# Two of the eight last output tiles made by POOL from a second laying-out of the roots, and the values of the second mixers turned three steps later

## The chip, the cores and the metric

The kernel runs on one core of one Trainium2 chip. The metric is device time in microseconds: lower is better. All times in this document are microseconds unless marked ns. The engines are PE (TensorE, matmuls; PEld are its weight loads), DVE (VectorE), ACT (ScalarE), POOL (GpSimd) and SP (SyncE, which issues most DMAs here).

## What is computed

Two transformer blocks in fp32 on 512 tokens of width 1024. The first is one layer: a mixer with windowed attention and neighborhood attention, then a squared-relu MLP. The second has two layers, each a half-step SwiGLU MLP, a mixer (`c0`, `c1`) of sliding-window attention with a sink beside a short convolution, and a second SwiGLU MLP. Two parts matter for this change, the attention's input and the last norm:

```python
h = rms_norm_2(x, mix_norm[l])
z = h @ w_in[l]
q, k, v = z[..., :Q_END], z[..., Q_END:K_END], z[..., K_END:V_END]
...
p = jnp.where(mask_b, jnp.exp(scores - m), 0.0)
out = jnp.einsum("bnkgqs,bnskd->bnqkgd", probs, v_band)
...
def rms_norm_2(x, gain):
    inv = lax.rsqrt(jnp.mean(x * x, axis=-1, keepdims=True) + NORM_EPS)
    return (x * inv) * gain
return rms_norm_2(x, final_norm)
```

## The kernel before

**Layout.** x lies in SBUF with the features on the partitions: eight tiles `x[:, m, :]` of 128 features by 512 tokens, and the output leaves in the same form. Every dense product is made of three passes per 128x128 piece of weights: w_hi by h_hi, w_hi by h_lo, w_lo by h_hi (lines 769 to 771, 128x512 each), where hi and lo are the two parts into which a value is split. A result is 8 such steps (24 matmuls) into one of three PSUM banks. Weights come by DMA in units of 512 KB; ACT makes w_hi (line 894), DVE makes w_lo (line 1091).

**What sets the order.** The class `Plan` writes one list of jobs, and each engine's program walks that list and emits its own part of each job, so every engine works strictly in list order. `dense` calls `next_slot` after each step, and `later(n, job)` puts a job n slots (steps of three matmuls) on. The engines are held together only by semaphores.

**The second mixers.** `second_mixer` begins with `qkv_gqa(s, 9)`: a result for the keys (`stack` k), one for the values (`project_v`), and four for the queries (`stack` 0 to 3). For each stack DVE scales the bank by the root of the norm into a buffer z (line 1083), ACT copies two or four halves as the high part (line 940), and DVE subtracts them for the low part (line 1158). For the values DVE scales into z (1083), PE turns z by four transposes of 128x128 against the identity into a bank (job `v_turn`, line 833), and ACT copies that bank to v (line 956). The second argument of `qkv_gqa`, 9, is the number of slots from the end of the values' result to the turn. PE's transposes wait for the semaphore `evacuated` of the values' z. In the second mixers' attention PE makes scores (line 783) into two banks in turn, and DVE takes them out with the distance bias (line 1270, semaphore `biased`); the third score of a group waits until the first is taken out.

**The end.** Job `output`: PE sums the squares of each token into four columns (lines 854, 857), ACT takes the root (`token_root`, line 1052), DVE inverts it (1305) and spreads it by the identity into four 128x128 blocks of a z (1310). PE multiplies each block by ones (line 862), which lays the inverse roots out over all partitions in a PSUM bank, `score_bank[0]`. DVE then makes the eight output tiles in place, x times gain times that bank (line 1314), and SP issues one DMA of 256 KB for each as its tile is ready (line 1447). SP then waits until all have landed.

Of the kernel before, what the change touches and what calls it, by code (L numbers as in the profile page):

```python
# [32 lines left out]
Z_RING = 5  # L33
WARMING = 11
GRID_W = 64
GRID_R = TOKENS // GRID_W
# [71 lines left out]
class Plan:  # L108
# [20 lines left out]
        "neg_sinks": ("neg_sinks",), "rel_bias": ("rel_spread",), "far_1": (), "far_2": (),  # L129
        "warm_root": (), "output": ("norm_summed", "rooted", "inverted"),  # L130
    }
# [291 lines left out]
    def second_mixer(self, layer):  # L423
        s, name = 3 + 3 * layer, f"c{layer}"
        self.phase_result[s] = len(self.results) - 1
        self.add("far_2", layer)
        self.add("pad_conv", layer)
        self.pending_norm = s
        self.qkv_gqa(s, 9)
        self.split_job = "split_g"  # L430
        self.attend(name, 5, 10, 11)
        for f in range(4):
            key = (layer, f)
            self.add("conv_c", key, self.dense_h(s))
            r = self.dense_h(s)
            self.add("conv_h", key, r, self.z("conv_u", key))
            self.later(3, "conv_own", *key)
            self.later(5, "conv_earlier", *key)
            r = self.dense_h(s)
            self.add("conv_b", key, r, self.z("project_lo", key))  # L440
            self.later(3, "conv_hi", *key)
        self.finish_beside()
        self.split_job = "split_v"
        self.out_projection(("cat", layer), s + 1)
        self.pending_norm = s + 1
# [82 lines left out]
def two_blocks(nc, dram, out):  # L528
    stack = ExitStack()
    with stack:  # L530
# [85 lines left out]
        names = dict.fromkeys(name for of in Plan.SIGNALS.values() for name in of)  # L616
        signals = {name: signal(name) for name in [*names, "mm_done", "evacuated", "ones_set", "eps_set", "rel_cleared", "spread", "rms_spread", "output_done"]}
        landed = [signal(f"w_landed{i}", 16) for i in range(UNITS_HELD)]
# [129 lines left out]
        def tensor_program(engine):  # L748
# [4 lines left out]
            for job, key, r, zs in jobs:  # L753
# [96 lines left out]
                elif job == "output":  # L850
# [9 lines left out]
                    for b in range(BLOCKS):  # L860
                        pe.wait_ge(signals["spread"].s, b + 1)
                        engine.matmul(score_bank[0][:, block(b)], ones[:, :], z[zs[1] % Z_RING][:, block(b)],
                                      start=b == 0, stop=True, skip_group_check=True).then_inc(signals["rms_spread"].s, 1)

        v_result, v_buffer = {}, {}
# [4 lines left out]
        def scalar_program(engine):  # L870
# [13 lines left out]
            for job, key, r, zs in jobs:  # L884
# [165 lines left out]
                elif job == "output":  # L1050
                    act.wait_ge(*done("norm_summed", FINAL))
                    engine.activation(token_root[:, :], value_bank[:, 0:BLOCKS], ACT.Sqrt, bias=eps_col[:, :], scale=1 / D_MODEL).then_inc(signals["rooted"].s, 1)

        h_until, conv_buffer, merge_result = {}, {}, {}
# [16 lines left out]
        def vector_program(engine):  # L1071
# [21 lines left out]
            for job, key, r, zs in jobs:  # L1093
# [209 lines left out]
                elif job == "output":  # L1303
# [7 lines left out]
                    v.wait_ge(signals["rms_spread"].s, BLOCKS)  # L1311
                    for m in range(KT):
                        v.wait_ge(*x_is(FINAL, m))
# [21 lines left out]
        def gpsimd_program(engine):  # L1335
            pool = Once(engine)
            for job, key, r, zs in jobs:
# [34 lines left out]
                elif job == "mask_bias":  # L1372
# [9 lines left out]
                    for (a, b), sign, base, event in ((lower, 1, GRID_R - 1, "bias_half"), (upper, -1, (WIN_W - 1) * GRID_R, "bias_masked")):  # L1382
                        in_place = i == 1 and sign < 0
                        if sign < 0:
# [4 lines left out]
                                             pattern=[[0, 4], [sign * GRID_R, b - a], [0, GRID_R]], channel_multiplier=-sign).then_inc(signals[event].s, 1)  # L1389

                elif job == "merge_b":
                    m = key
# [15 lines left out]
        def sync_program(engine):  # L1408
# [18 lines left out]
            for job, key, r, zs in jobs:  # L1427
# [16 lines left out]
                elif job == "output":  # L1444
                    for m in range(KT):
                        sp.wait_ge(signals["output_done"].s, m + 1)
                        engine.dma_start(out[m * P:(m + 1) * P, :], x[:, m, :]).then_inc(out_stored.s, 16)
# [139 lines left out]
```

## Time and profile before

| | us |
|---|---|
| runs | 2527.48, 2526.25, 2525.29 |
| median | 2526.25 |
| profiled execution, whole | 2525.54 |
| profiled execution, span from first to last instruction | 2523.7 |
| PE busy in the span | 2496.8 (99%) |
| DVE, ACT, POOL busy | 1189.6, 947.5, 182.6 |
| mean granted TensorE clock | 0.998 |

The span is what the trace shows, and 1.84 of the profiled execution lie around it. A row of a timeline gives the start, the duration, the engine and line, output<-input, and in brackets how long the engine was idle before it and who released it. Rows of the chain of waits give start, length and what the end of the kernel hung on at that time. In the tables by stretch the granted clock is a share of full speed: 1.00 is 2.4 GHz and 0.50 is 1.2 GHz.

### The profile page before, as it was taken

Reading aid. Unit: us, or ns where it says so; the run is one execution under the profiler, and the core shown is the slowest. Engines: PE = TensorE matmul, PEld = TensorE weight load, DVE = VectorE, ACT = ScalarE, POOL = GpSimd, SP = SyncE. Lnnn points to the kernel's source line nnn. Section 1 sums busy time; section 2 is a strip of 40 time slices with the busy share of each in tenths; the row PEclk is TensorE's granted clock in tenths of the full one; section 3 lists DMA queues with packets and bytes.
Section 4 is the critical chain, followed back from the end, with each engine's and each line's share of the span. In section 5 each row is a group of like instructions: output and inputs, shape, how many; then the busy total and the mean of one; then the engine's idle time right before and its main releaser. Section 6 shows DMA issues by size and latency. Waiting matters only on the chain.

```text
span 2523.7 us, 28242 instructions
## 1 busy us (share of the span) xinstructions
PE 2496.8 (99%) x11504; PEld 2071.3 (82%) x11504; DVE 1189.6 (47%) x1595; ACT 947.5 (38%) x1398; POOL 182.6 (7%) x179
## 2 busy tenths in 40 slices
PE   9999999999999999999999999999999999999998
PEld 7878888888888888878888888888888788888887
DVE  6443454434475343454454444543444644544444
ACT  6668333322343232356432222422222464322222
POOL 2031010000020000011200000100000122000001
PEclk9999999999999999999999999999999999999999
DMA  7454433233223333245423332333332354332322
GB/s 197 109 124 118 134 108 100 92 100 101 92 84 109 93 99 94 89 130 130 115 95 100 93 99 89 99 97 99 94 101 87 112 142 117 100 99 93 100 90 78
DMA packets 78513, 265.33 MB, mean 105 GB/s; under 512 B 9648, under 2 KB 12976, under 8 KB 78000
## 3 DMA queue, kind: packets, MB, share of 16 engines
q1 hardware_dynamic: 69376, 233.57, 29.4%
q0 software_dynamic: 9008, 29.96, 6.0%
q8 instruction: 91, 1.49, 0.2%
q14 instruction: 38, 0.31, 0.0%
HBM read 234.56 MB, written 2.19 MB: 94 GB/s over the span
## 4 chain that ended last, share of the span: by engine, by line
PE 89%; DVE 4%; ACT 3%; issue 3%; POOL 0%; DMA 0%; SPq 0%; DVEq 0%; ACTq 0%; POOLq 0%
PE bank L769 28%; PE bank L770 28%; PE bank L771 28%; PE bank L810 2%; DVE w_lo L1091 2%; ACT w_hi L894 1%; PE bank L783 1%; PE bank L797 1%; DVE x L1207 1%; DVE z L1083 1%; ACT z L882 0%; POOL square_sum L1350 0%; DVE q L1158 0%; PE bank L843 0%; ACT h_hi L907 0%
## 5 line engine op out<-in xcount | busy, mean ns | idle before, releaser
L769 PE MATMUL bank<-h_hi,w_hi 128*128 128x512 f32 x2224 | 879.7, 396 | 2.7 <-DVE h_lo L1106 1.5
L771 PE MATMUL bank<-h_hi,w_lo 128*128 128x512 f32 x2224 | 867.2, 390 | 0.0
L770 PE MATMUL bank<-h_lo,w_hi 128*128 128x512 f32 x2224 | 867.0, 390 | 0.0
L1091 DVE TENSOR_TENSOR w_lo<-w_raw,w_hi 128x1024 fp32r<-128x1024 f32 (+2 forms) x392 | 485.3, 1239 | 318.3 <-ACT w_hi L894 317.9
L894 ACT ACTIVATE w_hi<-w_raw 128x1024 fp32r<-128x1024 f32 (+1 forms) x435 | 449.0, 1034 | 409.4 <-PE bank L771 407.3
L771 PEld LDWEIGHTS bank<-h_hi,w_lo 128*128 128x128 f32 x2224 | 417.9, 188 | 88.5
L769 PEld LDWEIGHTS bank<-h_hi,w_hi 128*128 128x128 f32 x2224 | 418.5, 188 | 86.9 <-DVE h_lo L1106 2.7
L770 PEld LDWEIGHTS bank<-h_lo,w_hi 128*128 128x128 f32 x2224 | 418.7, 188 | 80.8 <-issue 1.9
L769 PE MATMUL bank<-act_hi,w_hi 128*128 128x512 f32 x960 | 373.4, 389 | 0.0
L770 PE MATMUL bank<-act_lo,w_hi 128*128 128x512 f32 x960 | 373.4, 389 | 0.0
L771 PE MATMUL bank<-act_hi,w_lo 128*128 128x512 f32 x960 | 373.4, 389 | 0.0
L1083 DVE TENSOR_TENSOR z<-bank,rms_inv 128x512 f32<-128x512 f32 x238 | 168.6, 709 | 317.2 <-PE bank L771 316.1
L1207 DVE SCALAR_TENSOR_TENSOR x<-bank,x 128x512 f32<-128x512 f32 x152 | 104.6, 689 | 284.2 <-PE bank L771 284.2
L771 PEld LDWEIGHTS bank<-act_hi,w_lo 128*128 128x128 f32 x960 | 180.2, 188 | 37.5
L769 PEld LDWEIGHTS bank<-act_hi,w_hi 128*128 128x128 f32 x960 | 180.2, 188 | 37.5
L770 PEld LDWEIGHTS bank<-act_lo,w_hi 128*128 128x128 f32 x960 | 180.2, 188 | 37.1
L1350 POOL TENSOR_TENSOR square_sum<-square_sum,z 128x512 f32<-128x512 f32 x55 | 73.7, 1340 | 1839.5 <-ACT z L882 1839.5
L1014 ACT ACTIVATE act_hi<-z 128x512 fp32r<-128x512 f32 x88 | 55.6, 632 | 389.9 <-DVE z L1228 389.9
L1009 ACT ACTIVATE z<-z 128x512 f32<-128x512 f32 x88 | 55.6, 632 | 285.0 <-DVE z L1083 285.0
L1091 DVE TENSOR_TENSOR act_lo<-z,act_hi 128x512 fp32r<-128x512 f32 x120 | 83.1, 692 | 105.0 <-ACT act_hi L1014 61.4
L907 ACT ACTIVATE h_hi<-x,gains 128x512 fp32r<-128x512 f32 x56 | 40.6, 724 | 124.0 <-DVE x L1207 119.8
L1341 POOL DMA_DIRECT2D w_lo<-w_raw x51 | 44.3, 868 | 322.5 <-ACT w_lo L897 322.5
(169 smaller groups left out, 1676.8 us busy)
## 6 DMA issues: line engine op xcount, KB each, us to landing
w_raw<-ffn_wg_dram SPq DMA_DIRECT2D x88, 512.0 KB, 3.5
w_raw<-ffn_wu_dram SPq DMA_DIRECT2D x88, 512.0 KB, 3.5
w_raw<-w_in_dram SPq DMA_DIRECT2D x67, 512.0 KB, 3.6
w_raw<-ffn_wd_dram SPq DMA_DIRECT2D x64, 512.0 KB, 3.5
w_lo<-w_raw POOLq DMA_DIRECT2D x51, 512.0 KB, 4.4
w_raw<-w_up_dram SPq DMA_DIRECT2D x32, 512.0 KB, 3.5
w_raw<-w_down_dram SPq DMA_DIRECT2D x32, 512.0 KB, 3.5
w_raw<-w_out_dram SPq DMA_DIRECT2D x24, 512.0 KB, 3.5
```

Of the source, the lines that this page charges most:

```text
L769: engine.matmul(to, w_hi[s][:, lhs], hi, start=k == 0, stop=False)
L770: engine.matmul(to, w_hi[s][:, lhs], lo, start=False, stop=False)
L771: product = engine.matmul(to, w_lo[s][:, lhs], hi, start=False, stop=job == "k_last")
L810: product = engine.matmul(value_bank[:, half(place(name, h))], turned[0:rows, n * P:(n + 1) * P], values[name][0:rows, chunk, value_head(n ...
L894: engine.activation(w_hi[s][:, 0:width], w_raw[s][:, 0:width], ACT.Copy).then_inc(signals["w_hi"].s, 1)
L1009: engine.activation(z[zs[1] % Z_RING][:, :], z[zs[0] % Z_RING][:, :], ACT.Silu).then_inc(signals["silued"].s, 1)
L1014: engine.activation(act_hi[:, plan.hidden[key] % FF_RING, :], z[zs[1] % Z_RING][:, :], ACT.Copy).then_inc(signals["act_hi"].s, 1)
L1083: engine.tensor_tensor(to, src, scale, ALU.mult).then_inc(signals["evacuated"].s, 1)
L1091: engine.tensor_tensor(lo, value, hi.bitcast(F32), ALU.subtract).then_inc(signals[event].s, 1)
L1207: engine.scalar_tensor_tensor(x[:, m, :], dense_bank[plan.results[r].bank][:, :], factor(r), x[:, m, :], ALU.mult, ALU.add).then_inc(signa ...
L1341: engine.dma_start(w_lo[s][:, 0:width].bitcast(F32), w_raw[s][:, 0:width], accum_op=ALU.add).then_inc(signals[f"w_added{s}"].s, 16)
L1350: engine.tensor_tensor(to, to, z[zs % Z_RING][:, :], ALU.add).then_inc(signals["scaled_sum" if scaled else "square_sum"].s, 1)
```

## The change

Two independent edits. In the second mixers the turn of the values is put 12 slots behind their result, not 9. In the job `output`, after the four matmuls that lay the roots out for DVE, PE does the same four once more into `turn_bank[0]` and signals `rms_for_pool`. ACT, after its root, multiplies tiles 0 and 1 of x by their gains in place (`gained`), then copies the second bank to the SBUF tensor `rms_inv` (`root_copied`). POOL multiplies these two tiles by `rms_inv`, DVE makes only tiles 2 to 7, and SP issues the eight stores in the order 2, 3, 0, 4, 5, 1, 6, 7, each when its tile is signalled. The lines of the changed kernel are one to twenty further down (833 becomes 834, 862 becomes 863, 1314 becomes 1325, 1447 becomes 1467).

```diff
+BY_POOL = 2
@@ second_mixer
-        self.qkv_gqa(s, 9)
+        self.qkv_gqa(s, 12)
@@ tensor_program, job "output", behind the four matmuls of line 862
+                    pe.wait_ge(*turn_freed(len(plan.turns) - 1))
+                    pe.wait_ge(*turn_freed(len(plan.turns) - 2))
+                    for b in range(BLOCKS):
+                        spread = engine.matmul(turn_bank[0][:, block(b)], ones[:, :], z[zs[1] % Z_RING][:, block(b)],
+                                              start=b == 0, stop=True, skip_group_check=True)
+                    spread.then_inc(signals["rms_for_pool"].s, 1)
@@ scalar_program, job "output", behind the root
+                    for m in range(BY_POOL):
+                        engine.activation(x[:, m, :], x[:, m, :], ACT.Copy, scale=gains[:, 9, m:m + 1]).then_inc(signals["gained"].s, 1)
+                    act.wait_ge(signals["rms_for_pool"].s, 1)
+                    engine.activation(rms_inv[:, :], turn_bank[0][:, :], ACT.Copy).then_inc(signals["root_copied"].s, 1)
@@ vector_program, job "output"
-                    for m in range(KT):
+                    for m in range(BY_POOL, KT):
@@ gpsimd_program
+                elif job == "output":
+                    pool.wait_ge(*done("root_copied", FINAL))
+                    for m in range(BY_POOL):
+                        pool.wait_ge(signals["gained"].s, m + 1)
+                        engine.tensor_tensor(x[:, m, :], x[:, m, :], rms_inv[:, :], ALU.mult).then_inc(signals["output_done_g"].s, 1)
@@ sync_program, job "output"
-                    for m in range(KT):
-                        sp.wait_ge(signals["output_done"].s, m + 1)
+                    for m in (2, 3, 0, 4, 5, 1, 6, 7):
+                        if m < BY_POOL:
+                            sp.wait_ge(signals["output_done_g"].s, m + 1)
+                        else:
+                            sp.wait_ge(signals["output_done"].s, m - BY_POOL + 1)
                         engine.dma_start(out[m * P:(m + 1) * P, :], x[:, m, :]).then_inc(out_stored.s, 16)
```

On PE, in the mixer of the second block's first layer, the result that begins below is that of the second stack of queries. Before, with the semaphores that each row waits for:

```order
L769 MATMUL bank<-h_hi,w_hi 128x512 [waits evacuated,w_lo_v]
L770 MATMUL bank<-h_lo,w_hi 128x512
L771 MATMUL bank<-h_hi,w_lo 128x512
L769 MATMUL bank<-h_hi,w_hi 128x512
L770 MATMUL bank<-h_lo,w_hi 128x512
L771 MATMUL bank<-h_hi,w_lo 128x512
L833 MATMUL bank<-identity,z 128x128 [waits evacuated]
L833 MATMUL bank<-identity,z 128x128 x3
L769 MATMUL bank<-h_hi,w_hi 128x512
```

The four transposes stand behind the result's second step. In the changed kernel the same place, from the result's third step on:

```order
L770 MATMUL bank<-h_hi,w_hi 128x512
L771 MATMUL bank<-h_lo,w_hi 128x512
L772 MATMUL bank<-h_hi,w_lo 128x512
L770 MATMUL bank<-h_hi,w_hi 128x512
L771 MATMUL bank<-h_lo,w_hi 128x512
L772 MATMUL bank<-h_hi,w_lo 128x512
L770 MATMUL bank<-h_hi,w_hi 128x512
L771 MATMUL bank<-h_lo,w_hi 128x512
L772 MATMUL bank<-h_hi,w_lo 128x512
L834 MATMUL bank<-identity,z 128x128 [waits evacuated]
L834 MATMUL bank<-identity,z 128x128 x3
L770 MATMUL bank<-h_hi,w_hi 128x512
```

Nine matmuls now stand ahead of the transposes that stood behind them; the wait goes with the transposes. In the order of the work of ACT, DVE and POOL in the mixers nothing moves, the copy to v included.

On SP, the last rows of the program, the eight stores; before:

```order
L1417 DMA w_raw<-ffn_wd_dram 128x768 [waits w_lo_v] x8
L1447 DMA out_dram<-x 128x512 [waits output_done] x8
L530 UNCONDITIONAL_BRANCH [waits out_stored]
```

and in the changed kernel, where output_done comes from DVE and output_done_g from POOL:

```order
L1434 DMA w_raw<-ffn_wd_dram 128x768 [waits w_lo_v] x8
L1467 DMA out_dram<-x 128x512 [waits output_done] x2
L1467 DMA out_dram<-x 128x512 [waits output_done_g]
L1467 DMA out_dram<-x 128x512 [waits output_done] x2
L1467 DMA out_dram<-x 128x512 [waits output_done_g]
L1467 DMA out_dram<-x 128x512 [waits output_done] x2
L531 UNCONDITIONAL_BRANCH [waits out_stored]
```

The third store and the sixth now wait for POOL, with DVE's tiles queued behind them.

## Rows read from the trace of the kernel before

**Rows 1.** The page: busy us by engine, share of the span, instructions
```profile
PE 2496.8 (99%) x11504; PEld 2071.3 (82%) x11504; DVE 1189.6 (47%) x1595; ACT 947.5 (38%) x1398; POOL 182.6 (7%) x179
```
**Rows 2.** PE's waits: who for whom, total, times, longest
```profile
PE bank L783 <- DVE neg_max L1270: 7.6, 6, 3.5
PE bank L833 <- DVE z L1083: 2.1, 2, 1.0
```
**Rows 3.** Timeline, mixer of the second block's first layer, around the turn
```profile
1099.08 0.39 PE L771 MATMUL bank<-h_hi,w_lo 128*128 128x512 f32 x1
1099.74 0.69 DVE L1083 TENSOR_TENSOR z<-bank,rms_inv 128x512 f32<-128x512 f32 x1
...
1100.49 0.66 PE L833 MATMUL bank<-identity,z 128*128 128x128 f32 x4 [1.02 <-DVE z L1083]
...
1104.46 0.58 ACT L956 ACTIVATE v<-bank 128x512 f32<-128x512 f32 x1
...
1122.71 0.33 PE L783 MATMUL bank<-k_hi,q 128*128 128x128 f32 x1 [0.64 <-DVE neg_max L1270]
```
**Rows 4.** Chain of waits, same mixer: start, length, what the end hung on
```profile
1099.02 0.69 DVE k_lo L1158
...
1103.50 1.07 ACT w_hi L894
...
1121.58 0.69 DVE q L1158
...
1122.30 0.35 DVE probs L1270
```
**Rows 5.** PE's waits in the second layer's mixer, 1980 to 2100
```profile
PE bank L783 <- DVE neg_max L1270: 0.7, 1, 0.7
```
**Rows 6.** Timeline of PE: two long waits in the first mixer
```profile
53.71 0.38 PE L783 MATMUL bank<-ka_hi,qa 128*128 128x256 f32 x1 [3.48 <-DVE neg_max L1270]
104.30 0.66 PE L797 MATMUL bank<-identity,probs 128*128 128x128 f32 x4 [1.67 <-ACT probs_t L1038]
```
**Rows 7.** By stretch: time, busy of PE PEld DVE ACT POOL, clock, DMA share, GB/s
```profile
55.00:56.00 1.00, 0.89 (x3) 0.89 (x4) 0.52 (x5) 0.98 (x2) 0.13 (x1) 0.50 0.31 61
...
58.00:59.00 1.00, 1.00 (x5) 0.79 (x4) 0.00 (x0) 1.00 (x5) 0.00 (x0) 0.81 0.92 180
105.00:110.00 5.00, 5.00 (x34) 4.47 (x33) 3.81 (x9) 3.96 (x9) 0.86 (x1) 1.00 0.33 66
2515.80:2516.00 0.20, 0.13 (x2) 0.00 (x0) 0.03 (x1) 0.00 (x0) 0.00 (x0) 0.93 0.00 0
2517.30:2517.60 0.30, 0.00 (x0) 0.00 (x0) 0.30 (x2) 0.00 (x0) 0.00 (x0) 0.50 0.02 7
2519.00:2520.00 1.00, 0.00 (x0) 0.00 (x0) 1.00 (x3) 0.00 (x0) 0.00 (x0) 0.50 1.06 410
2522.60:2522.80 0.20, 0.00 (x0) 0.00 (x0) 0.00 (x0) 0.00 (x0) 0.00 (x0) 0.50 1.13 440
```
**Rows 8.** Timeline of the end, all engines
```profile
2513.76 0.26 ACT L1052 ACTIVATE token_root<-bank,eps_col 128x4 f32<-128x4 f32 x1 [1.14 <-PE bank L857]
...
2514.80 1.13 PE L862 MATMUL bank<-z,ones 128*128 128x128 f32 x8 [1.08 <-DVE z L1310]
2515.97 5.36 DVE L1314 SCALAR_TENSOR_TENSOR x<-x,gains,bank 128x512 f32<-128x512 f32 x8 [0.73 <-PE bank L862]
2516.74 4.94 SPq L1447 DMA_DIRECT2D out_dram<-x  x8
```
**Rows 9.** Line 1447: issue ns min/median/max, starts; us to landing
```profile
L1447 SPq DMA_DIRECT2D out_dram<-x x8: 332/333/348, 2516.7 to 2521.4; - x8
...
DMA to landing us min/median/max: 2.0/2.0/2.0
```
**Rows 10.** Groups by line: prices of the like work on ACT and POOL
```profile
L977 ACT ACTIVATE conv_y<-conv_u,conv_w 128x512 f32<-128x512 f32 x8 | 5.7, 708 | 0.0
L1406 POOL TENSOR_TENSOR z<-z,conv_y 128x512 f32<-128x512 f32 x8 | 10.3, 1289 | 37.5 <-DVE z L1083 37.5
```

More of the change, by code:

```diff
@@ L129 @@
         "neg_sinks": ("neg_sinks",), "rel_bias": ("rel_spread",), "far_1": (), "far_2": (),
-        "warm_root": (), "output": ("norm_summed", "rooted", "inverted"),
+        "warm_root": (), "output": ("norm_summed", "rooted", "inverted", "root_copied"),
     }
@@ L616, in two_blocks @@
         names = dict.fromkeys(name for of in Plan.SIGNALS.values() for name in of)
-        signals = {name: signal(name) for name in [*names, "mm_done", "evacuated", "ones_set", "eps_set", "rel_cleared", "spread", "rms_spread", "output_done"]}
+        signals = {name: signal(name) for name in [*names, "mm_done", "evacuated", "ones_set", "eps_set", "rel_cleared", "spread", "rms_spread", "rms_for_pool", "gained", "output_done", "output_done_g"]}
         landed = [signal(f"w_landed{i}", 16) for i in range(UNITS_HELD)]
```

## The prediction

> **What bounds the kernel now.** I read the page first. PE is busy for 2496.8 of 2523.7 [rows 1], so outside the last few microseconds time can come only from PE's waits or its work. The next view is the one of PE's waits, since it names what the first edit aims at: the transposes of line 833 wait twice for DVE's z (line 1083), 2.1 together, 1.0 the longest [rows 2]. Those are the turns of the values in the two second mixers. The same view has line 783 (scores) waiting for DVE's exit from the score banks, 7.6 in 6 waits. Two of these six turn out to matter: 0.64 at 1122.71, in the same mixer and 22 after the turn [rows 3], and 0.7 in the other layer's [rows 5]. So the third step was the chain of waits between the two places, and the fourth the timeline of the end. There PE has finished and the path is root, laying-out, eight DVE products, stores, landing [rows 8, 9].
>
> **Edit 1, the turn three steps later.** It adds and removes no instruction. Before, PE has nothing left to do in front of the transposes from 1099.47 (the last matmul starts at 1099.08 and takes 0.39) and waits 1.02 until z is out at 1100.43 (1099.74 + 0.69) [rows 3]. Now nine matmuls stand ahead. By the page a matmul costs 2496.8 / 11504 = 0.22 [rows 1], since they overlap, so they fill about 2.0, and PE reaches the transposes near 1101.4, 0.9 after z is there. This wait goes, and the transposes' own 0.66 stays as it is. PE is then 1.0 ahead of where it stood. The copy to v on ACT stands at the same place in ACT's order and started at 1104.46 [rows 3], long after either time of the turn, so it does not move.
>
> What is late next? The chain of waits answers it. From 1099 to 1122 it does not run over PE at all: DVE's low parts of the keys, ACT's w_hi, DVE's low parts of the queries, one after the other on DVE and ACT with gaps of hundredths between them, up to DVE's exit of the first score at 1122.30 (0.35) [rows 4]. None of these instructions waits for the turn, and none is held by a matmul of this stretch: each result was finished before DVE came to it. So the chain does not move when PE comes earlier. Its end releases PE's third score at 1122.71, where PE already waits 0.64 [rows 3]. With PE 1.02 earlier, this wait becomes 0.64 + 1.02 = 1.66 and ends at the same instant, and behind it everything is where it was. In the second layer's mixer it is the same, 0.7 + 1.0 = 1.7 [rows 2, 5]. **The first edit is worth 0 in each mixer.** What would hide the turn is thus worth nothing as long as DVE and ACT are behind. Bounds: 1.0 per mixer gained, 2.1 in all, if PE's lead were kept [rows 2]; and a loss if the longer wait costs PE its clock, which is a rival below.
>
> **Edit 2, the end.** Removed: two of DVE's eight products. Eight take 5.36, one every 0.67 [rows 8], so DVE ends 1.33 earlier. Whether the kernel does hangs on the stores. Before, issues go from 2516.74 to 2521.4, one every 0.66, each lands after 2.0 [rows 8, 9], and the span ends 0.3 after the last landing (2521.35 + 2.0 + 0.35 = 2523.7).
>
> Two readings of these stores are possible. Landing stays at 2.0 from the first to the last, as if the DMA engines kept up with DVE and had room. But the DMA share is 1.06 at 410 GB/s while stores come every 0.66, and 262 KB every 0.66 is 397 GB/s [rows 7]. A single stretch of 0.2 has 440. I take it that the DMA engines are as good as full and drain one tile in 0.66; the other end of the bound, 0.60, is from the 440 (262 / 440). Data flow begins near 2517.6, 0.86 after the first issue (the share in 2517.30 to 2517.60 is 0.02) [rows 7], and landing follows the end of a tile's data by 2.0 - 0.86 - 0.66 = 0.5. If that is so, eight tiles need 5.3 of continuous flow, which is what they get before. Then the change cannot make the end earlier; it can only open a gap.
>
> The Trainium skill, DMA: Bandwidth & Descriptors, Specifications, gives a fabric ceiling of 435 GB/s and a limit of about 358 GB/s for a core's HBM traffic. The 410 of this trace is above the second, so here the measurement decides; by the first a tile would take 0.60, and the sum below would be 0.4 smaller.
>
> The gap comes from POOL's tile, third in SP's order. Its path, from rows of like work:
> - PE's second laying-out starts behind the first, which ran from 2514.80 for 1.13 [rows 8]: eight passes (two to each matmul), one every 0.12 with a last one of 0.28. At full speed the second eight would end at 2515.93 + 0.97 = 2516.9. But the granted clock is 0.93 over the stretch 2515.80 to 2516.00 and 0.50 from then on [rows 7], after five microseconds in which PE was busy about half the time. What PE did up to that fall is the same in the changed kernel, so I expect it at the same instant: two passes at full speed, six every 0.24, and an end at about 2517.6.
> - ACT's two gain products, 0.71 each as in line 977 [rows 10], run from 2514.02 (2513.76 + 0.26) to 2515.5, beside PE: cost 0 [rows 8]. ACT's copy from the bank is like line 956, 0.58 [rows 3]: 2517.6 to 2518.25.
> - POOL's two products are like line 1406, 1.29 each [rows 10]: 2518.3 to 2519.6 and to 2520.9.
>
> SP stores tile 2 at 2516.74 and tile 3 at 2517.40. Then it stands on tile 0 until 2519.65, while tiles 4 to 7 (ready from 2518.1, the last at 2520.1) are queued behind it. Data of two tiles end at 2518.9, and the flow resumes at 2519.65 + 0.86 = 2520.5. Six tiles at 0.66 take 3.96, to 2524.5; with landing 0.5 and the end 0.35 the span is 2525.3, which is **1.6 later** than 2523.7. With 0.60 to a tile it is 1.2 later. With PE at full clock the tile of POOL is ready at 2518.9 and all is 0.7 earlier: 0.9 or 0.5 later. If the DMA engines have room beyond any of this, the issues decide: tiles 4 and 5 at 0.37 each behind tile 0, tile 1 at 2520.95, 6 and 7 at 2521.3 and 2521.7, landed 2523.7, span 2524.05, 0.35 later; with the full clock as well, 0.4 earlier. So edit 2 lies between -0.4 and +1.6. I take **+1.5**, near the end that both rows (the clock's fall, the DMA share) point to.
>
> **Sum.** 0 + 0 + 1.5 on the profiled execution: 2525.5 + 1.5 = 2527.0. That execution is 0.7 below the median of the three runs (2526.25), so the same on the median is 2527.75. Before's own runs spread over 2.2, so this difference is smaller than what one can tell from three runs.
>
> **The rivals.**
> - *The change does what it is made for.* PE keeps its lead in both mixers (-2.0) and DVE's shorter list moves the last store (-1.3): 2522.9. For it: the two waits are there, and landing is a constant 2.0. Against it: the chain between the turn and the scores runs over DVE and ACT alone [rows 4]. Chance 0.06.
> - *The lead is kept, the end is as forecast.* That is so if some matmul of this stretch does hold DVE or ACT: -2.0 + 1.5, 2525.7. Chance 0.08.
> - *The end is not bound by the DMA engines*, or POOL's tile comes early, with edit 1 at 0: -0.4 to +0.5, about 2526.3. For it speaks the constant landing of 2.0. Chance 0.17.
> - *Slower, by the clock.* In each second mixer PE's two waits (1.0 and 0.6) become one of 1.7 at 1121. After a wait of 3.48, ended at 53.71, the clock stood at 0.50 in 55 to 56 and came back inside 58 to 59 [rows 6, 7], about 3.3 at half speed, a loss of 1.7. Twice that is 3.4: 2526.25 + 3.4 + 1.5 = 2531.2. Against it: a wait of 1.67 at 104.30 left the clock at 1.00 [rows 6, 7]. It decides somewhere between a wait of 1.67 and one of 3.48, and mine are 1.66 and 1.7. Chance 0.04.
>
> **How the numbers follow.** The forecast, edit 1 at 0 and the end +0.5 to +1.6, has 0.65. The predicted time is 2527.7. The range takes in the forecast, the second and the third rival with half of before's spread around them: 2524.6 to 2529.3; the first rival and the fourth are outside, 0.10, and the rest is what runs scatter. About 0.2% (5.05) is what a measurement of this kernel can tell from no change. Below 2521.2 lies nothing but the first rival with scatter: 0.02. Above 2531.3 lies half of the fourth: 0.02. All else, 0.96, is within 0.2%.
>
> **What would show it.** Edit 1: line 834 no longer waits, and the third score's wait on DVE's exit is about 1.7 in both mixers, ending at the same time as before (1122.7); it is wrong if that wait stays at 0.6 and its time is 1.0 earlier. Edit 2: the second laying-out takes nearer 1.7 than 1.0, POOL's first product ends at about 2519.6, SP stands for some 2 behind the second store, the DMA share is 0 for about 1.6 in the middle and 1.0 to the end, and the last stores take longer than 2.0 to land. It is wrong if they still land in 2.0 with issues 0.37 apart, for then the engines had room. The whole is wrong if a wait not seen before appears on PE outside these two places.

## The result, and the profile after

| | before | after |
|---|---|---|
| median of 17 runs each | 2525.83 | 2530.31 |
| lowest to highest | 2524.79 to 2528.39 | 2529.17 to 2533.34 |
| profiled execution, time | 2525.5 | 2532.92 |
| its span | 2523.7 | 2530.0 |
| mean granted clock | 0.998 | 0.995 |

After over before is 1.0019, 95% interval 1.0012 to 1.0027: slower by 4.5, where I had forecast 1.45 and a range that ended at 2529.3. The profiled execution of the kernel after is 2.6 above its median, so its trace shows more than the 4.5: its span is 6.3 longer than before's, 0.4 of it ahead of the second mixers, 3.2 in them and 2.7 at the end. Of the eleven executions of two kernels among the experiments below, one took 5107.76 (e9) and one 4206.40 (e10), a slow state that no other run here shows, and the figures of e9 and e10 are of the other ten.

PE's waits in the kernel after (waiter, what it waits for: total, times, longest), against [rows 2]:

```profile
PE bank L784 <- DVE neg_max L1281: 9.9, 5, 3.5
```

The wait of the transposes (line 834 now) is gone, as intended. The scores' wait has grown from 7.6 to 9.9, by more than the 2.1 that were removed. The timeline around the turn and the third score, against [rows 3], and the same score in the second layer's mixer:

```profile
1101.77 0.60 PE L834 MATMUL bank<-identity,z 128*128 128x128 f32 x4
...
1123.11 0.33 PE L784 MATMUL bank<-k_hi,q 128*128 128x128 f32 x1 [1.87 <-DVE neg_max L1281]
...
2021.12 0.33 PE L784 MATMUL bank<-k_hi,q 128*128 128x128 f32 x1 [1.89 <-DVE neg_max L1281]
```

This mixer begins at 1086.50 here and at 1086.09 before (start of the matmul that sums the squares of its norm), so 1123.11 is 1122.70 on before's scale: the wait does end at the same instant as before, 1122.71. The chain of waits in front of it is the one of [rows 4], link by link:

```profile
1121.98 0.69 DVE q L1169
1122.67 0.03 issue
1122.70 0.35 DVE probs L1281
1123.05 0.02 DVE neg_max L1281
...
1123.11 0.44 PE bank L784 x2
```

What is new comes behind it. The stretches from 1123 on (busy us of PE PEld DVE ACT POOL, granted clock, DMA share, GB/s); before, the clock is 1.00 in all of them, as in this one:

```profile
1125.00:1126.00 1.00, 1.00 (x6) 0.83 (x5) 0.00 (x0) 0.98 (x2) 0.63 (x1) 1.00 0.98 197
```

and after:

```profile
1123.00:1124.00 1.00, 0.89 (x5) 0.80 (x6) 0.74 (x7) 1.00 (x2) 0.28 (x1) 1.00 0.00 0
1124.00:1125.00 1.00, 1.00 (x6) 0.86 (x5) 0.97 (x4) 0.97 (x2) 0.62 (x1) 0.68 0.00 0
1125.00:1126.00 1.00, 1.00 (x3) 0.76 (x3) 0.06 (x1) 0.98 (x2) 0.24 (x1) 0.50 0.98 197
1126.00:1127.00 1.00, 1.00 (x4) 0.76 (x3) 0.00 (x0) 0.99 (x2) 0.64 (x1) 0.50 0.98 197
1127.00:1128.00 1.00, 1.00 (x4) 0.77 (x3) 0.00 (x0) 1.00 (x7) 0.00 (x0) 0.61 1.03 197
```

PE's clock is at its lower level, 1.2 GHz, for (0.32 + 0.50 + 0.50 + 0.39) x 2 = 3.4, and PE is busy all that time. The same stretch from 1125 holds three matmuls in place of six, so half of these 3.4 is lost, 1.7. The mixer as a whole, from its norm's matmul to that of the MLP behind it, is 174.05 before and 175.65 after; the second layer's 174.02 and 175.63. The MLPs between and behind the mixers differ by 0.01 at most, so these two mixers hold 3.2 of the difference.

At the end of the profiled execution, against [rows 8]:

```profile
2518.63 2.05 PE L863 MATMUL bank<-z,ones 128*128 128x128 f32 x8 [1.08 <-DVE z L1321]
2520.47 1.91 PE L868 MATMUL bank<-z,ones 128*128 128x128 f32 x8
2520.71 4.04 DVE L1325 SCALAR_TENSOR_TENSOR x<-x,gains,bank 128x512 f32<-128x512 f32 x6 [1.65 <-PE bank L863]
2521.49 5.71 SPq L1467 DMA_DIRECT2D out_dram<-x  x8
2522.42 0.60 ACT L1063 ACTIVATE rms_inv<-bank 128x512 f32<-128x512 f32 x1 [3.35 <-PE bank L868]
2523.09 2.49 POOL L1406 TENSOR_TENSOR x<-x,rms_inv 128x512 f32<-128x512 f32 x2 [9.56 <-ACT rms_inv L1063]
```

The stretches of the stores, SP's wait, and landing, against [rows 7, 9]:

```profile
2523.00:2524.00 1.00, 0.00 (x0) 0.00 (x0) 1.00 (x2) 0.01 (x1) 0.91 (x1) 0.50 0.70 268
2524.00:2525.00 1.00, 0.00 (x0) 0.00 (x0) 0.75 (x2) 0.00 (x0) 1.00 (x2) 0.50 0.00 0
2525.00:2526.00 1.00, 0.00 (x0) 0.00 (x0) 0.00 (x0) 0.00 (x0) 0.58 (x1) 0.50 0.80 307
2526.00:2527.00 1.00, 0.00 (x0) 0.00 (x0) 0.00 (x0) 0.00 (x0) 0.00 (x0) 0.50 1.04 404
...
SPq L1467 <- POOL x L1406: 1.9, 1, 1.9
...
DMA to landing us min/median/max: 2.0/2.4/2.9
```

SP stands 1.9 for POOL's tile, the DMA engines run dry for about 1.5 (0.3 of the first of these stretches, the whole second, 0.2 of the third), and from then to the end they are full. In this execution the clock was at 0.50 already in front of the first laying-out (2.05, not 1.13), so that its end is long even for the changed kernel: 15.39 from the first matmul of the last norm to the end of the span, against 12.73 before.

### The profile page after: what moved, and what is told of

Its sections match the earlier page's. It is cut to its first block, busy times and chain, and to the rows that moved or that the text cites. A ratio compares the mean times of both kernels' runs of the same rounds, so it can differ in the third digit from the quotient of the medians.

```text
span 2530.0 us, 28262 instructions
## 1 busy us (share of the span) xinstructions
PE 2502.5 (99%) x11512; PEld 2076.4 (82%) x11512; DVE 1188.5 (47%) x1593; ACT 949.3 (38%) x1401; POOL 185.2 (7%) x181
## 4 chain that ended last, share of the span: by engine, by line
PE 88%; DVE 4%; ACT 3%; issue 3%; POOL 1%; DMA 0%; SPq 0%; POOLq 0%; ACTq 0%; DVEq 0%
PE bank L770 28%; PE bank L772 28%; PE bank L771 28%; PE bank L811 2%; DVE w_lo L1102 1%; ACT w_hi L901 1%; PE bank L784 1%; PE bank L798 1%; DVE x L1218 1%; DVE z L1094 1%; ACT z L889 0%; POOL square_sum L1361 0%; DVE q L1169 0%; ACT h_hi L914 0%; PE bank L844 0%
```

## The experiments

Theory A, made after the result: the long single wait of PE in front of the third score costs the clock, and that is all that edit 1 does to the time. Theory C, the prediction's own: the last stores are bound by the DMA engines, at about 0.66 a tile. Each expectation was written before its run. "Mixer" is the time between the two marks named above, from the run's trace. Medians are of 11 executions (ten in e9 and e10, one in e13 and e14) against 15 to 33 of the kernel before on the same chip; those medians of before are 2525.3 to 2525.6, their spans' 2523.5 to 2523.7. Where the interval of a ratio takes in 1, the whole times alone do not tell the kernel from the one before. The argument then goes by the mixers: in the five traces in which nothing in them was changed (before, e2, e5, e6, e12) they take 174.02 to 174.05, so 0.1 is a difference there.

### The two edits apart: e1 and e2

e1 is the kernel before with this line alone:

```diff
-        self.qkv_gqa(s, 9)
+        self.qkv_gqa(s, 12)
```

> Only the values' turn is put 12 slots behind its result in the second mixers; the end is as before. Theory A (the merged wait costs the clock): PE's third score in each second mixer waits 1.9 instead of 0.6, the turn waits 0, the granted clock falls to 0.50 for about 3.3 us shortly behind that wait in both mixers, and each costs 1.7 us: the kernel is about 3.4 us slower than before (+2.5 to +3.6). Theory B (the loss is all in the new end): 0 us, within 0.3 of before.

Measured: 2528.54, ratio 1.0012 (1.0003 to 1.0020). The span's median is 3.0 longer, the mixers take 175.61 and 175.64, the wait is 1.87 in both, and behind each the clock is at 0.50 for 3.4:

```profile
1122.49 0.33 PE L783 MATMUL bank<-k_hi,q 128*128 128x128 f32 x1 [1.87 <-DVE neg_max L1270]
```

e2 is the changed kernel with the turn back at 9.

> Only the end is changed (POOL makes tiles 0 and 1); the turn stands at 9 as before. Theory A: +1.0 to +1.7 us, from the gap in which SP stands behind the second store for POOL's first tile, with the DMA engines idle for 1 to 1.6 us in the middle; the clock in the second mixers is 1.00 throughout. Theory B (the loss is all in the new end): +4.5 us. If POOL's tiles are worth what they are made for: -1.3 us.

Measured: 2527.35, ratio 1.0008 (0.9999 to 1.0017), 1.8 slower by the medians. Mixers 174.05 and 174.03. The span is 1.4 longer; the rest is time outside the span, whose median is 2.1 here and 1.8 in the kernel before. The two edits apart give 3.0 + 1.8 = 4.8, together they gave 4.5; within the scatter that is the same, so nothing else is needed to explain the result. In e2's profiled execution the clock held until both layings-out were done:

```profile
2514.65 1.13 PE L863 MATMUL bank<-z,ones 128*128 128x128 f32 x8 [1.08 <-DVE z L1321]
2515.61 1.06 PE L868 MATMUL bank<-z,ones 128*128 128x128 f32 x8
...
SPq L1467 <- POOL x L1406: 1.1, 1, 1.1
```

SP stands 1.1, not 1.9, and from the last norm's first matmul (2510.85; 2511.01 before) to the end of the span it takes 13.45, where before took 12.73: 0.7 more. With the clock down in front of the first laying-out the like footing is e7, e9, e10 and e14, whose end is the old one: there it is 13.65 to 13.84, and the kernel after has 15.39, which is 1.6 to 1.7 more. So the new end costs 0.7 or some 1.6, by where the clock falls.

### Is it the idle time, and not the place of the turn: e4

The turn at 12, and in front of the third score six matmuls that nobody reads, which fill PE's idle time:

```diff
-        self.qkv_gqa(s, 9)
+        self.qkv_gqa(s, 12)
...
+                    if name in ("c0", "c1") and (i, g, n) == (0, 0, 2):
+                        pe.wait_ge(*done("rooted", {"c0": 3, "c1": 6}[name]))
+                        for _ in range(6):
+                            engine.matmul(value_bank[:, 0:P], ones[:, :], ones[:, :], start=True, stop=True)
```

> The turn at 12 as in the changed kernel, the end as before, and ahead of the third score in each second mixer PE makes six matmuls of 128x128 of ones by ones (12 passes of 0.12 us, 1.4 us) into a bank that is free there; they are extra work inside the wait and nothing reads them. Theory A: PE's idle time there falls from 1.9 to about 0.4, the clock stays at 1.00, and the kernel is within 0.3 us of before, 3.4 faster than with the turn at 12 alone. If the clock falls for another reason than PE's idleness, it is +3.4 as without the filling.

Measured: 2525.24, ratio 0.9998 (0.9989 to 1.0007); the wait 0.55 in both mixers, clock 1.00, mixers 174.00 and 174.06. The first of them:

```profile
1120.15 1.50 PE L780 MATMUL bank<-ones 128*128 128x128 f32 x12
1122.21 0.33 PE L787 MATMUL bank<-k_hi,q 128*128 128x128 f32 x1 [0.55 <-DVE neg_max L1274]
```

Matmuls whose result nobody reads give back what e1 lost (2525.24 against 2528.54). The turn is at 12 in both kernels, and only PE's idle time was taken away, so it was the cause. It also shows the first step of the prediction apart: with the clock held, the turn at 12 is worth 0.

### How long an idle time does it take: e8, e3, e9, e13, e10, e14

e8 puts the turn at 10.

> Only the turn moves, one slot later than before (10). PE waits about 0.35 us at the transposes and 1.3 to 1.5 at the third score in both second mixers, all told what it was. Theory A2 (the clock is kept as long as one wait stays at or under 1.7): 0 us, clock 1.00 in both mixers. If what matters is that most of the idle time stands at the scores: +3 us, with the clock at 0.50 behind them.

```profile
1100.10 0.66 PE L833 MATMUL bank<-identity,z 128*128 128x128 f32 x4 [0.36 <-DVE z L1083]
...
1122.32 0.33 PE L783 MATMUL bank<-k_hi,q 128*128 128x128 f32 x1 [1.36 <-DVE neg_max L1270]
```

Measured: 2525.22, ratio 0.9999 (0.9990 to 1.0008), clock 1.00, mixers 174.07 and 174.04. A wait of 1.36 (1.35 in the second mixer) costs nothing.

e3 puts the turn at 8.

> Only the turn moves, one slot earlier than before (8). PE then reaches the transposes 0.7 us earlier and waits 1.7 there, and its third score's wait shrinks from 0.64 to 0 or nearly. The sum of the two waits is the same 1.7. Theory A1 (one long wait anywhere costs the clock): the clock falls behind the turn in both mixers, +2.5 to +3.5 us. Theory A2 (a wait of up to 1.7 leaves the clock, as the 1.67 wait of the first mixer did; only 1.87 and more do not): 0 us, clock 1.00. Theory A3 (the clock falls only because of where the scores stand, not for the wait's length): 0 us.

Measured: 2526.87, ratio 1.0005 (0.9996 to 1.0014), the span 1.3 longer. The wait at the turn was 1.70 and 1.72 and the clock stayed at 1.00. But the score's wait was 0.59, where I expected it gone, and the mixers took 174.69 and 174.65. The chain of waits says why: ACT's order changed with the job.

```profile
1102.52 0.60 ACT v L956
1103.11 0.03 issue
1103.14 1.07 ACT w_hi L894
```

The copy to v now stands ahead of w_hi. This mixer began at 1085.11, so w_hi starts at 1104.12 on before's scale, against 1103.50 in [rows 4]: 0.62 later, and the mixers lost 0.64 and 0.63. The DVE and ACT chain sets the mixer's length, in this direction too.

e9 is e4 with one such matmul in place of six.

> The turn stands at result 12 and one extra product of 128 by 128 (of ones, into a bank that is free there; it changes nothing that is computed) stands in front of the third score, where six stood in the run before. The last result is made from the stack as in the kernel before. Theory A (one long idle time in front of the third score costs the clock): one product takes about 0.2 off the idle time of 1.87 to 1.89, so about 1.65 is left, which lies under the 1.70 that the run with the turn at 8 bore at full clock. If the length of the one idle time is what decides, wherever it stands, the clock stays at 1.00 and the time is that of before, 2525.5 (2524.8 to 2526.2). If it is also the place that decides (the softmax stretch, with short products before and after the score), the clock still falls after the score and the time stays at 2528.5.

Measured: 2528.02, ratio 1.0010 (1.0001 to 1.0020). The score's wait was 1.68 in both mixers. The first took 174.02 with its clock at 1.00, the second 175.67 with a fall:

```profile
2018.00:2019.00 1.00, 0.78 (x4) 0.71 (x5) 0.73 (x7) 1.00 (x2) 0.10 (x1) 1.00 0.00 0
2019.00:2020.00 1.00, 1.00 (x5) 0.93 (x4) 0.85 (x4) 0.97 (x2) 0.78 (x1) 0.61 0.00 0
2020.00:2021.00 1.00, 1.00 (x4) 0.71 (x4) 0.34 (x3) 0.98 (x2) 0.07 (x1) 0.50 0.78 156
```

The same wait, in the same code of the two layers, with two outcomes. The next run is this kernel once more.

> The kernel of e9 once more, for its trace alone. There, with an idle time of 1.68 in both second mixers, the clock fell in the second and not in the first. Theory D (with this idle time it is decided anew in each execution) expects any of the four cases, and a case other than e9's shows it. Rival (each place has its own bound, the second mixer's lower): first mixer 174.0 at clock 1.00, second 175.7 with a fall, as in e9.

Measured: waits 1.66 and 1.63, and both mixers lost their clock: 175.61 and 175.62. In its first mixer:

```profile
1123.00:1124.00 1.00, 1.00 (x6) 0.81 (x5) 0.95 (x3) 0.97 (x2) 0.83 (x1) 0.69 0.00 0
1124.00:1125.00 1.00, 1.00 (x4) 0.84 (x4) 0.53 (x4) 0.98 (x2) 0.07 (x1) 0.50 0.47 94
```

A bound that hangs on the place alone falls with this: the first mixer kept its clock in e9 and lost it here. e13 ran on another chip than e9, and these two traces alone do not tell a difference of chips from one of executions; for the second speaks that e9's ten spans, all on one chip, lie over 4.0 (2.5 in the kernel before on that chip).

e10 puts the turn at 7.

> The turn stands at result 7 in the second mixers, the last result is made as before. The wait in front of the turn was 1.02 at result 9 and 1.70 at result 8, and it should be 2.3 to 2.4 at result 7, in both mixers. Theory A with a bound between 1.70 and 1.87 expects that the clock falls to 0.50 right behind the turn, for some 3 us in each mixer. What that costs differs from the case of turn 12: behind this turn TensorE runs weight-like products of the next results and then waits again for the score, so part of the lost 1.6 us can be taken back out of later waits; I expect mixers 0.6 to 2.2 us longer than before each, of which 0.6 is ScalarE's copy to v that goes ahead of w_hi, as at result 8: time 2527 to 2530. Rival (the clock falls only where an idle time stands in the softmax stretch): clock 1.00 in both mixers, 2526.9 as at result 8.

Measured: 2528.16, ratio 1.0011 (1.0002 to 1.0020). Waits at the turn 2.38 and 2.41; the first mixer took 174.48 at clock 1.00, the second 176.03:

```profile
1101.19 0.66 PE L833 MATMUL bank<-identity,z 128*128 128x128 f32 x4 [2.38 <-DVE z L1083]
...
1998.01 1.12 PE L833 MATMUL bank<-identity,z 128*128 128x128 f32 x4 [2.41 <-DVE z L1083]
```

The four transposes take 0.66 or 1.12: in the second mixer the clock fell inside the wait. The ten spans of this kernel lie in three heaps, five of 2524.9 to 2525.5, four of 2527.1 to 2527.9, one of 2529.4. I read them as none, one or both of the mixers having lost their clock, but the heaps are about 2 apart where a lost clock costs the mixer 1.55 (176.03 - 174.48), and the one traced span (2527.8) also has 0.9 from the clock at the end (13.65 against 12.73), so the spans do not show it.

> The kernel of e10 once more, for its trace alone. There, with 2.38 and 2.41 in front of the turn, the clock held in the first mixer (174.5) and fell in the second (176.0). Theory D expects that the case can differ this time; its spans, in three heaps near 2525.1, 2527.6 and 2529.4, say that none, one or both mixers lose 2. Rival (bound by place): the same case as in e10.

Measured: waits 2.40 and 2.38, mixers 174.48 and 175.99, the same case as in e10. So e10 and e14 do not tell the theories apart: in front of the turn a bound by place is still possible.

What the traces show together, of waits in front of the third score: at 1.36, none of 2 lost the clock; at 1.63 to 1.68, 3 of 4; at 1.87 to 1.89 (after and e1), 4 of 4. In front of the turn: at 1.70 and 1.72, none of 2; at 2.38 to 2.41, 2 of 4, both in the second mixer. The wait of [rows 6] in the first block, 1.67 or 1.68, stands in all 17 traces and lost the clock in none. So the length alone does not decide: 1.63 in front of a score lost it, 2.40 in front of a turn kept it. What else decides is open.

### Does the wait only move: e7

The turn at 12 and the first scores three slots later, so that they are ready when PE comes:

```diff
-        self.qkv_gqa(s, 9)
+        self.qkv_gqa(s, 12)
...
-        self.attend(name, 5, 10, 11)
+        self.attend(name, 8, 10, 11)
```

> Turn at 12, and the whole attention of the second mixers three slots later (first score at 8 slots, not 5), the end as before. PE then comes to the third score 2 us later, when DVE has taken the first out. Theory A (DVE's and ACT's chain holds PE only there, and PE's idleness costs the clock): no wait of PE at turn or scores in these mixers, clock 1.00, and the 1.7 to 2.0 us of waiting in each mixer are gained: -2.5 to -3.5 us against before, if the attention still ends ahead of the output projection. Rival: the attention, 2 us later, ends behind the last result of the convolution and PE waits there instead: -1 to +1 us.

Measured: 2527.05, ratio 1.0005 (0.9997 to 1.0014); clock 1.00, mixers 174.55 and 174.56. PE's waits in the first of them, the one for the norm's sum aside, which every kernel has (0.3):

```profile
PE bank L769 <- DVE q L1091: 0.6, 1, 0.6
PE bank L783 <- DVE neg_max L1270: 0.5, 1, 0.5
PE bank L769 <- DMA w_lo<-w_raw: 0.4, 1, 0.4
```

The long wait and the fall are gone, but nothing is gained: three waits, 1.5 together, take the place of before's two (1.66), and each mixer is 0.5 longer. One of 0.5 is still at the third score; one is for a DMA of weights; the one of 0.6 is at the output projection, for the attention's result (`q`, at 1212.56), which is the rival's mechanism. By the medians the kernel is 1.5 slower, above the rival's range of -1 to +1 too.

### Where the chain can be shortened: e11 and e15

If DVE and ACT set the length, the gain lies in their order. Before, they make the next result's w_hi and w_lo behind the stack of queries; here, ahead of it. e11 has the turn at 10, e15 at 12:

```diff
+        self.split_slots = 0
-        self.qkv_gqa(s, 9)
+        self.qkv_gqa(s, 12)
+        self.split_slots = 1
...
-            self.next_unit(r)
+            self.next_unit(r, self.split_slots)
```

> In the two second mixers the split of the next result's weights (w_hi on ScalarE, w_lo on VectorE) is queued ahead of the turning stack's own work on those engines, and the turn stands at result 10; the last result is as before. Chain theory: the mixers end when VectorE's and ScalarE's chain lets them, and TensorE's waits are only its shadow. With the split first, TensorE's products of the next result start earlier, the chain per result gets shorter than TensorE's own 5.4 us, and the waits at the turn and at the score go: 1 to 1.6 us less per mixer, 2522.3 to 2523.5. Rival B (the chain only moves: the stack's work comes later by what the split took, and the turn or the score waits for that instead): within 0.5 of before, 2525 to 2526. Rival C (the stack's results come so late that a bank isn't free): slower than 2526.5, with a new wait of TensorE on a bank.

Measured: 2524.21, ratio 0.9994 (0.9985 to 1.0002), mixers 172.98 and 172.99, waits 0.3 at the turn and 0.3 at the score. The mixers are 1.1 and 1.0 shorter, as expected; the median is 1.3 less than before's, not the 2.0 to 3.2 that I expected, and its interval takes in 1.

> As e11, with the turn at 12 as in the change. With the split first the waits at the turn and at the third score were 0.3 and 0.3. Chain theory: joined, they make one of at most 0.7, under all that cost the clock, so that the turn at 12 is worth 0 here as I had forecast for the change: mixers 173.0, clock 1.00, 2524.2 (2523.5 to 2524.8). Rival (turning at 12 is dear in itself, through VectorE's or ScalarE's order, not through the wait): mixers 0.5 or more above 173.0.

Measured: **2522.49, ratio 0.9988 (0.9979 to 0.9997)**, 2.8 faster than before by the medians, and so some 7.3 faster than the change, of which it leaves out the new end (1.8). Mixers 172.39 and 172.42. Beside the norm's 0.3 only this is left of the waits in either of them:

```profile
PE bank L786 <- DVE neg_max L1273: 0.3, 1, 0.3
```

ACT's w_hi of two results in a row, in the kernel before and then in e15:

```profile
1109.29 1.06 ACT L894 ACTIVATE w_hi<-w_raw 128x1024 fp32r<-128x1024 f32 x1
...
1115.08 1.06 ACT L894 ACTIVATE w_hi<-w_raw 128x1024 fp32r<-128x1024 f32 x1
```

```profile
1109.50 1.06 ACT L897 ACTIVATE w_hi<-w_raw 128x1024 fp32r<-128x1024 f32 x1 [1.22 <-PE bank L774]
...
1114.94 1.06 ACT L897 ACTIVATE w_hi<-w_raw 128x1024 fp32r<-128x1024 f32 x1 [1.22 <-PE bank L774]
```

5.79 per result before, 5.44 now, and ACT now waits for PE: PE sets the pace (24 matmuls, one every 0.227, are 5.4). I had expected the same 173.0 as in e11, a turn at 12 being worth 0. It is worth another 0.6 per mixer: the turn's wait of 0.3 is gone and the score's has not grown, so here PE's lead is kept. What edit 1 was made for thus needs the split's order first.

### The end: e5, e6, e12

e5 is e2 with POOL's two tiles stored last:

```diff
-                    for m in (2, 3, 0, 4, 5, 1, 6, 7):
+                    for m in (2, 3, 4, 5, 6, 7, 0, 1):
```

> As the run with only the new end (turn at 9), but SP stores tiles 2 to 7 first and POOL's tiles 0 and 1 last. Theory C (the DMA engines are full from the second store on, at 0.65 us a tile, and the loss of the new end is the gap in which SP stands for POOL): with no gap the last store lands where it does in the kernel before, so span +0.0 to +0.3 us. Theory D (the engines have room and DVE sets the pace): -0.5 us or better. What lies outside the span was 1.8 us before and 1.8 to 3.6 with POOL's products: if POOL causes that, it stays above 1.84 here; if the queued-up stores do, it is back at 1.84.

Measured: 2526.22, ratio 1.0002 (0.9993 to 1.0011); the span's median 0.4 longer than before's (0.3 was the most I expected; nothing was gained either), landing 2.0 to 2.4. Its stretches show no gap and no room:

```profile
2517.00:2518.00 1.00, 0.00 (x0) 0.00 (x0) 1.00 (x3) 0.50 (x1) 0.42 (x1) 0.50 1.02 397
...
2520.00:2521.00 1.00, 0.00 (x0) 0.00 (x0) 0.00 (x0) 0.00 (x0) 0.07 (x1) 0.50 1.04 397
2521.00:2522.00 1.00, 0.00 (x0) 0.00 (x0) 0.00 (x0) 0.00 (x0) 0.00 (x0) 0.50 1.06 412
```

The last tile was made at 2520.1, but data flowed at the old rate until 2522.

e6 is the kernel before with its first store held until four tiles are made:

```diff
-                        sp.wait_ge(signals["output_done"].s, m + 1)
+                        sp.wait_ge(signals["output_done"].s, max(m, 3) + 1)
```

> The kernel before, with SP's first store held until DVE has made four tiles (2.0 us later); POOL makes none. Theory C (DMA engines full at 0.65 us a tile): data flow starts 2.0 us later and runs 5.2 us without a break, the last landing takes 3 us or more, span +1.9 us. Theory D (room in the engines): the issues catch up at 0.37 each, the last two stores go at DVE's pace, landing stays at 2.0 to 2.4, span +0.3 us or less. Outside the span: above 1.84 if queued-up stores cause it, 1.84 if POOL does.

Measured: 2527.49, ratio 1.0008 (0.9999 to 1.0016), the span 2.0 longer: the whole delay of the first store (3 x 0.67) comes through, though from then on SP could issue a store every 0.35 to 0.57. Issues, and landing:

```profile
L1447 SPq DMA_DIRECT2D out_dram<-x x8: 347/452/572, 2520.7 to 2524.2; - x8
...
2524.00:2525.00 1.00, 0.00 (x0) 0.00 (x0) 0.00 (x0) 0.00 (x0) 0.00 (x0) 0.50 1.07 410
...
DMA to landing us min/median/max: 2.0/2.7/3.0
```

Issued 3.5 apart from first to last (4.7 before), they land later and later. Theory C holds: the constant landing of 2.0 in [rows 9] was two equal rates, DVE's 0.67 and the DMA engines' 0.65, not spare room.

e12 is the kernel before with two products of POOL, of the size of the change's, that nobody waits for; they ran at 2518.74 and 2520.08 for 1.27 each.

> The kernel before, with two products on GpSimd of the size of the change's, of data that nobody reads any more, started once three of the last tiles are made. Nothing waits for them. It asks where the time outside of the span comes from, 1.8 in every kernel without such products and 2.1 to 2.4 in the median of those with them. If it comes from GpSimd having worked just ahead of the end, the time outside goes to 2.1 or more and the time to 2525.9 to 2526.3, with a span as before (2523.7). If it comes from the stores that wait for GpSimd, the time outside stays at 1.8 and the time at 2525.5.

Measured: 2525.98, ratio 1.0000 (0.9991 to 1.0009), time outside the span 1.82. The added time outside does not come from POOL having worked late, nor from stores that queue up (1.79 in e6). It appears in the three kernels whose stores wait for POOL's tiles (medians of 2.41 in after, 2.13 in e2, 2.09 in e5) and in no other. Its cause stays open.

## Why the prediction was wrong

- **What bounds the kernel: right.** From 1099 to 1122 DVE and ACT set the end (e3 and e4 from one side, e15 from the other), and the last stores are bound by the DMA engines (e5, e6).
- **The wait at the turn goes, PE's lead is lost at the third score, which starts at the same instant: right.** Line 834 does not wait, and the score starts within 0.01 of where it did. The rivals that keep the lead, 2522.9 and 2525.7, fall.
- **"0.64 + 1.02 = 1.66": the size was off.** It is 1.87 and 1.89. An idle time in the timeline counts from the modelled end of the last matmul, which is 0.39 long, while the next could have started 0.23 behind its start; so each row leaves out 0.16. PE really lost 1.18 + 0.80 = 1.98 before and loses 2.02 now (1123.11, less 1120.86, the start of the last matmul ahead of it, less 0.23), and only one 0.16 is left out of it. Two waits that are joined give more than the sum of their rows.
- **"The first edit is worth 0 in each mixer": the step that failed.** It costs 1.6 in each, by the clock, which the sum put at nothing. The mechanism stood among the rivals, with 3.4 for both mixers (3.2 measured) and 2531.2 for the kernel (2530.3), but at a chance of 0.04. What I held against it was one wait of 1.67 that had kept the clock [rows 6], read as a safe bound, with "mine are 1.66 and 1.7" set just under or on it. Both halves failed: mine were longer, and e9 and e13 lost the clock in 3 of 4 waits of 1.63 to 1.68. One instance at 1.67 and one at 3.48 left the outcome between them open, and a chance near even would have been the honest one.
- **Edit 2: right in mechanism, and in size in part by luck.** +1.5 forecast; the span's median is 1.4 longer in e2, and 0.3 is added outside the span, which no term had. SP stands 1.9 ("some 2"), the gap of the DMA engines is 1.5 (1.6), landing grows from 2.0 to 2.9. But I expected the clock to fall "at the same instant" as before, between the two layings-out, with the second at 1.7, and it does not: it fell ahead of both in the kernel after (the second took 1.91) and behind both in e2 (1.06). In e2 the end is 0.7 longer than before, where the prediction's case of full clock had 0.9; in the kernel after it is 1.6 to 1.7 longer than ends at the same clock. The 1.4 of the median lies between such cases.
- **Sum.** 2525.83 + 3.2 + 1.8 = 2530.8, measured 2530.31. The range left out the first rival and the fourth, and the time lies near the fourth. Its upper end was also drawn loosely: the highest case (+1.6) and half of before's spread (1.1) give 2528.95, not 2529.3; the time lies outside either.

The Trainium skill, TensorE: Matmul & The Clock Gate, A second HAM failure mode: psum-queue depth-cycling, tells that short idle stretches of PE, if they are frequent, make its clock go back and forth. Here a single one did, of 1.87, between stretches in which PE was never idle.

## What to carry to other kernels

Before taking a wait away from PE, look for the wait behind it on the same engine: if DVE or ACT sets the end, the two merge into one, the row is longer than the sum of both, and two harmless short waits can become one behind which the clock halves. Here two short idle times were better than one long one (0.36 and 1.36 in e8 against 1.87 in e1); where a long one can't be avoided, six matmuls without use in it cost nothing and kept the clock (e4), and one was not enough (e9, e13). And ask first for the order of the engine that sets the pace (e15): only behind that does PE's lead count. Stores that land in a constant time show that their rate is met, not that there is room.

## What the runs showed of the hardware

- PE's clock fell to its lower level behind single idle times from 1.63 up, not at each one (1.67 in the first block kept it in 17 of 17 traces), and not always at the same moment: inside the wait of 2.41 (e10), 1.0 behind the end of one of 1.68 (e9), 1.25 behind that of one of 1.87 (after; the 0.68 of its stretch makes 0.64 at the lower level). In the second mixers it came back after 3.4 each time, and the mixer was 1.5 to 1.7 longer. After the wait of 3.48 to 3.51 in the first block it was down for 3.4 in 14 traces and for 6.8 in three (after, e6, e13).
- The same code lost the clock in one trace and kept it in another (e9, e13), and a kernel with such waits scatters more: e9's spans lie over 4.0, those of e4, with the wait filled, over 1.1.
- At the end PE does the same in before, e6 and e12, and the laying-out took 1.13, 2.04 and 1.96, by where the clock fell. On one chip it took 1.13 in e1 and e4 and 1.87 in e3, on another 1.13 in e8 and 2.05 in e7. A single profile of an end is no measure of it.
- Eight stores of 256 KB left at 0.65 each, 397 to 414 GB/s, as long as one was waiting: with the stores held (e6) or DVE done earlier (e5) they left no faster.
